# A two-block transformer kernel in eleven stages: products of the identity with itself on TensorE at the changes of stage

## The reference

```python
# first block
h = _rms_norm(x, pre_norm_g)
z_q, z_kv, z_kr, g_attn, u_ssm, g_ssm = split(h @ w_in)
attn = _rms_norm(_mla_attention(z_q, z_kv, z_kr, ...), attn_out_g) * silu(g_attn)
ssm = gelu(_s5_bidirectional(u_ssm, ...))
ssm = _rms_norm(ssm * sigmoid(ssm @ w_glu + b_glu), ssm_out_g) * silu(g_ssm)
x = x + _rms_norm(concat([attn, ssm]) @ w_out, post_norm_g)
# second block (its projections, attention, retention and output product), then
h = modulated(_rmsnorm(x))
p_g, group = top_1(softmax(h @ w_grp + b_grp)); two experts of that group, by softmax
y = sum over the two of weight * ((silu(h @ w_gate[e]) * (h @ w_up[e])) @ w_down[e])
out = _rmsnorm(x + gate * y) * final_g
```

## Time and profile before

| | |
|---|---|
| median of 3 runs | 4364.99 us (4360.97 to 4367.25) |
| the profiled execution | 4367.83 us, its span 4366.0 us |
| mean granted TensorE clock | 0.959 of full |
| busy: PE, DVE, ACT, POOL | 92%, 68%, 56%, 28% |
| PE instructions | 21445 products, as many weight loads |
| from TensorE's last product to the meeting, and from there to the next product | up to 19.2 us together |

### The profile page before, as it was taken

One profiled execution on the slowest core, in us unless ns is written; L12 is line 12 of the kernel. 1 busy time (PEld: TensorE's weight loads), 2 busy tenths in 40 slices (PEclk: granted clock), 3 DMA queues, 4 the chain that ended last, 5 costly groups with the idle time before them and its releaser, 6 DMA issues. The chain is left out here.

```text
span 4366.0 us, 61138 instructions
## 1 busy us (share of the span) xinstructions
PE 4022.8 (92%) x21445; PEld 3412.4 (78%) x21445; DVE 2973.9 (68%) x3831; ACT 2433.6 (56%) x3867; POOL 1231.3 (28%) x846
## 2 busy tenths in 40 slices
PE   8989799999897997999799999997698799999995
PEld 8978689888776876888678888886687588888872
DVE  6667555555486884444477777774655799999985
ACT  6733333333323554333388888887422577777773
POOL 0000145445300110000288888884000111111114
PEclk9999899999998998999899999998899799999998
DMA  6666733333496433222440000004543688888987
GB/s 230 219 212 235 230 113 110 104 118 111 145 287 195 138 105 124 67 67 67 106 163 15 15 23 15 15 10 150 195 155 111 227 319 318 316 321 326 377 318 303
DMA packets 417337, 728.63 MB, mean 167 GB/s; under 512 B 121744, under 2 KB 314384, under 8 KB 396304
## 3 DMA queue, kind: packets, MB, share of 16 engines
q1 hardware_dynamic: 382560, 642.02, 43.0%
q10 hardware_dynamic: 20640, 50.87, 3.3%
q0 software_dynamic: 13968, 33.58, 2.0%
HBM read 601.84 MB, written 213.91 MB: 187 GB/s over the span
## 5 line engine op out<-in xcount | busy, mean ns | idle before, releaser
L2675 POOL TENSOR_TENSOR a_PL<-a_PT,a_PH 128x512 fp32r<-128x512 f32 x512 | 674.4, 1332 | 133.5 <-ACT a_PH L2794 130.3
L2844 DVE TENSOR_REDUCE a_part<-a_pA 128x1 f32<-128x1024 f32 (+1 forms) x384 | 360.0, 955 | 95.4 <-PE a_pA L2698 90.9
L2792 ACT ACTIVATE a_PT<-a_pB 128x512 f32<-128x512 f32 x576 | 340.7, 592 | 78.6 <-PE a_pB L2721 77.3
L2794 ACT ACTIVATE a_PH<-a_PT 128x512 fp32r<-128x512 f32 x576 | 364.4, 633 | 18.4
L3478 POOL DMA_INDIRECT w_XG<-between_h,all_slots x65 | 120.8, 1858 | 779.0 <-PE e_pT L3760 724.8
L1397 ACT ACTIVATE a_PT<-a_pT 128x512 f32<-128x512 f32 x128 | 69.5, 594 | 409.0 <-PE a_pT L1327 409.0
L1432 DVE TENSOR_REDUCE a_maxima<-a_pS 128x1 f32<-128x512 f32 x256 | 176.0, 689 | 132.6 <-PE a_pS L1309 131.1
L1341 PE MATMUL a_pO<-a_V,a_PT 128*128 128x128 f32 x2048 | 249.4, 275 | 1.0 <-DVE a_PT L1445 1.0
L1341 PEld LDWEIGHTS a_pO<-a_V,a_PT 128*128 128x128 f32 x2048 | 243.4, 192 | 6.5 <-DVE a_PT L1445 1.2
L1239 POOL TENSOR_TENSOR a_QL<-a_RQ,a_QT 128x512 fp32r<-128x512 f32 x16 | 20.5, 1284 | 800.6 <-DVE a_QP L1467 800.6
L2739 PE MATMUL a_pO<-a_PL,a_VH 128*128 128x512 f32 x576 | 225.7, 392 | 3.1 <-DVE a_PL L2854 2.1
(11 more groups left out here) (651 smaller groups left out, 10617.5 us busy)
## 6 DMA issues: line engine op xcount, KB each, us to landing
w_gate<-in_moe_w_gate SPq DMA_DIRECT2D x47, 2048.0 KB, 7.7
w_up<-in_moe_w_up SPq DMA_DIRECT2D x47, 2048.0 KB, 12.4
w_down<-in_moe_w_down SPq DMA_DIRECT2D x46, 2048.0 KB
between_yb<-e_Y ACTq DMA_DIRECT2D x46, 512.0 KB, 7.0
a_row_w<-in_w_ada SPq DMA_DIRECT2D x16, 1024.0 KB, 5.5
between_x<-m_X SPq DMA_DIRECT2D x32, 512.0 KB, 2.8
between_yb<-a_zeros SPq DMA_DIRECT2D x32, 512.0 KB, 14.6
between_tv<-pz_OV SPq DMA_DIRECT2D x16, 576.0 KB, 2.9
```

The costliest lines, as they stand in the source:

```text
L2675: pool.tensor_tensor(PL[:, t % RING, :], PT[:, t % RING, :], PH[:, t % RING, :].bitcast(F32), ALU.subtract).then_inc(S["p_low"], 1)
L2792: act.activation(PT[:, t % RING, :], pB[t % 2][:], ACT.Exp, scale=scale).then_inc(S["p_ready"], 1)
L2794: act.activation(PH[:, t % RING, :], PT[:, t % RING, :], ACT.Copy).then_inc(S["p_high"], 1)
L2844: dve.tensor_reduce(part[:, h, r % (NG2 // G4):r % (NG2 // G4) + 1], src, AX_X, ALU.max).then_inc(S["maxed"], 1)
```

## The change

A helper `keep_busy(pe, bank, ident, n)` issues n float32 products of the identity by itself, 128x128 each, into a PSUM bank that is not in use there; nothing waits for them, they wait for nothing, and nobody reads them. Fifteen calls are put in. Seven stand at the head of a PE list, ahead of its first wait: `attention_1` 56, `mix_1` 50, `project_2` 8, `attention_2` 54, `retention` 22, `mix_2` 10, `dispatch` 42. Six stand at the end of a PE list: `project_u` 38, `project_z` 20, `attention_1` 24, `s5` 16, `attention_2` 30, `dispatch` 32. The other two (30 and 56) stand behind a `return` in the helpers `t_stores_before` of `project_2` and `after` of `mix_2`, and issue nothing. The thirteen live calls issue 402 products. No other engine's list changes.

```diff
--- before.py
+++ after.py
@@ -337,6 +337,7 @@
                     products(g, piece, (pU if piece < 2 else pG)[piece % 2], S["mm_u" if piece < 2 else "mm_g"])
                     if piece < GT and g + 1 < NGR:
                         transposed(GT * (g + 1) + piece)
+            keep_busy(pe, pT[0], C["ident"], 38)
 
         @block.scalar
         def _(act):
@@ -846,6 +847,7 @@
             heads(NT - 1)
             gate(NT - 1)
             rope_turned(NT - 1)
+            keep_busy(pe, pA, C["ident"], 20)
 
         @block.scalar
         def _(act):
@@ -1045,6 +1047,12 @@
 
 
 HIGH_BITS = -4096
+
+
+def keep_busy(pe, bank, ident, n):
+
+    for _ in range(n):
+        pe.matmul(bank[:, 0:P], ident[:], ident[:], start=True, stop=True)
 
 
 def high_part(dve, out, x):
@@ -1290,6 +1298,7 @@
 
         @block.tensor
         def _(pe):
+            keep_busy(pe, pO, C["ident"], 56)
             def scores(t, h, g):
                 u = unit(t, h)
                 m = groups[g][1]
@@ -1386,6 +1395,7 @@
             for steps in between:
                 of_unit_before(steps, tile_at(NT), 0)
             row(tile_at(NT - 1))
+            keep_busy(pe, pS[:, 0, :], C["ident"], 24)
 
         @block.scalar
         def _(act):
@@ -1772,6 +1782,7 @@
                         if g % 2:
                             within(h, g)
                         across(h, g)
+            keep_busy(pe, pW[0], C["ident"], 16)
 
         @block.scalar
         def _(act):
@@ -2143,6 +2154,7 @@
 
         @block.tensor
         def _(pe):
+            keep_busy(pe, pG, C["ident"], 50)
             def last_stage(t):
                 i, b = t.i, t.b
 
@@ -2284,6 +2296,7 @@
 
         def t_stores_before(i):
             return 16 * (T_STORES * (i + 1) - 2 * of_context(i))
+            keep_busy(pe, pG, C["ident"], 30)
 
         @block.gpsimd
         def _(pool):
@@ -2345,6 +2358,7 @@
 
         @block.tensor
         def _(pe):
+            keep_busy(pe, pR, C["ident"], 8)
 
             def turned(t):
 
@@ -2676,6 +2690,7 @@
 
         @block.tensor
         def _(pe):
+            keep_busy(pe, pO[0], C["ident"], 54)
             def free(c):
                 if c >= 2:
                     u, r = divmod(c - 2, TURNS)
@@ -2753,6 +2768,7 @@
                     apply(t - LAG)
             for t in range(STEPS - LAG, STEPS):
                 apply(t)
+            keep_busy(pe, pA[0][:, 0, :], C["ident"], 30)
 
         @block.scalar
         def _(act):
@@ -3175,6 +3191,7 @@
 
         @block.tensor
         def _(pe):
+            keep_busy(pe, pX[0], C["ident"], 22)
             def free(c):
                 if c >= 2:
                     h, r = divmod(c - 2, TURNS)
@@ -3274,6 +3291,7 @@
 
         def after(t):
             return Tile(t.i + 1, 1 - t.b, t.n + t.b)
+            keep_busy(pe, pX[0], C["ident"], 56)
 
         @block.gpsimd
         def _(pool):
@@ -3333,6 +3351,7 @@
 
         @block.tensor
         def _(pe):
+            keep_busy(pe, pL, C["ident"], 10)
 
             def transposed(t):
                 pe.wait_ge(S["xh_ready"], t.i + 1)
@@ -3545,6 +3564,7 @@
 
         @block.tensor
         def _(pe):
+            keep_busy(pe, pb, C["ident"], 42)
             pe.wait_ge(S["matrices"], 1)
             pe.wait_ge(S["chosen"], 1)
             m = MM[:].rearrange("p t e -> p (t e)")
@@ -3558,6 +3578,7 @@
                 for j in range(8 * q, 8 * q + 8):
                     mm = pe.matmul(ps[:, 0:NB + 1], in_row[:, j, :], in_block[:, j, :], start=j == 0, stop=j == 2 * NT - 1)
             mm.then_inc(S["listed"], 1)
+            keep_busy(pe, pw, C["ident"], 32)
 
         @block.vector
         def _(dve):
```

## The result

The changed kernel took 4374.1 us, the median of its executions, against 4362.82 us for the kernel before: a ratio of 1.0024, with a 95% interval of 1.0013 to 1.0036. Timed again with twelve executions it took 4376.43 against 4364.29, ratio 1.0024 (1.0014 to 1.0034). It is slower by some 11 us. The forecast was no measurable change, 4363.

A forecast was written before the change was run, and what follows sets the result against it. TensorE, busy 92%, has stage-change pauses the dummies cannot shorten, so only the clock could be won. Ten steps summed to -1.9 us from 4367.83, giving 4365.9; the runs' median being 2.8 lower, 4363 us, 8 in 10 within 4353 to 4371.

The forecast's parts named there:

- The price of a dummy: Time of one added identity product on TensorE: 0.23 us at full clock, 0.43 at half clock.
- Step 1: project_u to project_z: 38 dummies may hold the clock for project_z's first products, -1.5 us (bounds 0 and -2.8).
- the even chance: project_u to project_z: even chances that the clock is held, since a 2 to 3 us pause may or may not cost it.
- Step 2: project_z to attention_1: meeting and loads +1.2 us late, -0.4 from the clock, net +0.8 (bounds -0.6 and +9.7).
- Steps 3 to 6: Changes attention_1 to s5, to mix_1, to project_2, to attention_2: -0.8, 0, 0 and +0.5 us.
- Step 7: attention_2 to retention: 30 and 22 dummies hold the clock, retention's first work speeds up, -2.3 us (bounds 0 and -3.0).
- Step 8: retention to mix_2: a product 1.3 us late, but the clock returns earlier; net -1.0 us (bounds -1.5 and +1.3).
- step 9: mix_2 to dispatch: count products 1.0 us late, 0.5 of it returned; net +0.4 us (bounds -0.5 and +7.1).
- Step 10: dispatch to experts: 32 dummies end late and delay experts' start, products gain nothing; +2.0 us (bounds -4.5 and +5.8).
- the ceiling of 30.6 us: Behind eleven pauses TensorE works 61.3 us at half clock; a clock held up could give 30.6 us, 0.7% of the span.
- Rival A: The clock holds across all ten changes and TensorE paces what follows: -23.4 us, 4341.6 us; chance 0.08.
- Rival B: Dummies do not raise the clock, run at 0.43 us and overrun their pauses: +42.7 us, 4407.7 us; chance 0.05.

The follow-up runs named there:

- g4: The kernel before with only the 38 dummies behind project_u; 4369.2 us, ratio 1.0005.
- f2: The changed kernel with its first five calls alone (project_u, project_z, both of attention_1, s5); 4369.81 us, ratio 1.0017.
- h4: The kernel before with 10 dummies of 512 columns behind project_u alone, the work of the 38; 4363.8 us, ratio 0.9991.
- h1: The changed kernel with a never-taken branch of 402 dummies ahead of the loop in TensorE's program of experts; 4381.67 us, ratio 1.0037.
- g3: The changed kernel without the 20 dummies behind project_z and the 42 ahead of and 32 behind dispatch; 4378.07 us, ratio 1.0031.
- g1: The changed kernel with each call's n products of 128 columns replaced by n/4 of 512 columns; 4372.84 us, ratio 1.0018.
- g2: The changed kernel with each dummy replaced by four increments of a semaphore nobody reads; 4500.78 us, ratio 1.0307.
- f4: The kernel before with only the 30 dummies behind attention_2 and the 22 ahead of retention; 4367.02 us, ratio 1.0008.
- e2: The kernel before with only the 32 dummies behind dispatch's last products; 4365.56 us, ratio 1.0003.

## Why the prediction was wrong

By its steps, with what two profiles of the changed kernel and the single-cause runs showed:

- **The price of a dummy** (0.23 us, 0.43 at the lower level): right. 38 took 8.64 (8.7 forecast), 20 4.63 (4.6), 24 5.52 (5.5), 42 11.92 (12.0), 10 3.95 (4.3), 54 13.64 (14.8), 32 9.17 (9.7). Only the 8, wholly at the lower level, took 3.75, over their bound of 3.4.
- **Step 1**, -1.5: here the forecast failed first. The start is faster: the first cast comes 1.1 us earlier against the first product in both profiles of the changed kernel, no more than in the kernel before's second profile, but 2.7 in g4 and f2, where the clock held; the even chance was fair. But 2.7 to 3.0 us are lost behind it, which with h4's run (no such loss with the same work in 20 matmul records) is the instructions' doing: a piece of them arrives while a store of the stage is under way, and the store takes 4.5 us in place of 2.9. The step said that project_z's next products follow directly on its first, and had no term for the rest of the stage.
- **Step 2**, +0.8: the meeting was late by 1.5 and 1.7 (1.2 forecast). Attention_1 then took 2.1 us more in both profiles and in f2 and h1, 2.5 in g3, which lacks the 20. So this part is not the late meeting. Nor is it the wait for `a_PR`, though that is 5.26 us in place of 3.79 before: it ends 10.1 us behind the first product, against 10.4. Most of it, 1.6 us, is lost in the last 8 us of the stage, where the clock falls. Before and after (stretch, length, TensorE's busy time and records, granted clock, DMA share, GB/s):

```profile
1170.70:1178.70 8.00, 6.34 (x53) 1.00 0.74 253
1176.60:1184.60 8.00, 6.67 (x42) 0.79 0.99 330
```

The second profile of the kernel before has 0.79 there too, so this isn't the dummies' alone; it made it good at the stage's start, where the clock held and it was 1.8 us faster. In g1, with wide dummies, the clock stays at 1.00 and the stage is 2.1 us shorter. In g2, with as many instructions and no work, the stage takes what it took before, so the number of instructions is not shown to lengthen it. What makes the clock fall there stays open.
- **Steps 3 to 6**, -0.8, 0, 0, +0.5: nothing beyond the noise. The first product of attention_2 was 0.3 late in one profile and 1.8 in the other (1.7 forecast), and its window still shows 0.66, as the step had feared of so thin a stream.
- **Step 7**, -2.3: from first product to scan the changed kernel's first profile is faster by just that, 2.30 us, but its first product came 1.6 later on `r_V`, so that 0.7 was left; in the second the first product came 3.0 later and only 0.4 of it returned. The step missed that load as the next thing to be late, and that a piece of instructions can fall into its flight. Alone (f4) the pair is not faster.
- **Step 8**, -1.0, and **step 9**, +0.4: mix_2's first transpose 0.7 late behind the stage's start, its last product 0.8 and 1.6 earlier; dispatch's first product 0.7 and 1.1 late, 0.5 of it returned. Right.
- **Step 10**, +2.0: +1.37 and +1.57, and +1.39 alone in e2, all against the first profile of the kernel before; against its second 0.3 less. Right in kind, a little high.
- **What no step had**: experts. A term for it stands nowhere, neither in the sum nor among the rivals. It is 6.8 us by the averages above, the greatest part of the 11, and 8.4 between the two profiles of each kernel.

So the step that failed is one that all ten share. The sum goes over the changes of stage and counts for each how late the meeting comes and what the first products save. Everything behind them it takes as unchanged, at 0 and without a reason. The 1608 added instructions as such were taken to cost nothing beyond the dummies' own time. The runs showed 6.8 us in experts and some 3 in project_z that follow the instructions and not the work. With these two terms the forecast of -1.9 would have been +7.9.

The tally: 6.8 in experts, some 3 in project_z, 1.6 at attention_1's start and 2.1 within it, and 1.5 at experts' start are 15.0, where the medians differ by 11.3. These items are read from profiled executions, and those of the two kernels differ by 15.6 and 15.5. So the tally is a rough one, and what the faster starts gave back isn't measured by itself. Of the ceiling of 30.6 us that is little: most stages' starts are paced by loads and casts, as the forecast had it. Rival A needed TensorE to pace them. Rival B is refuted: the clock rose under the dummies wherever they were many (1.00 at 1389.20 and 3011.00). The Trainium skill's rule on products in transpose mode (TensorE: Matmul & The Clock Gate, Part 4) found no use here, since dummies are plain products, and no run here shows it.

## What to carry to other kernels

An instruction that does nothing is not free even where its engine is idle: it moves the whole stream behind it, and stages far away, bound by transfers, can pay. If a pause is to be filled at all, take few wide products, which did no harm in project_z, and not many narrow ones, which did, and only where the first work behind it waits for nothing but TensorE can it pay; here no such filling gained anything clear of noise. When a load or a store takes longer than before, look for a piece of instructions in its flight. When a stage that wasn't touched gets slower, compare the count of instruction pieces in the two profiles before looking for a cause in the stage, and time the edit again with padding that does no work.

## What was not expected of the hardware

A 16 KB piece of TensorE's instructions lengthens a transfer in whose flight it begins: a store of 576 KB from 2.9 to 4.5 us in the median (251 and 53 issues), a load of 1152 KB from between 5.3 and 6.0 to between 7.2 and 9.5 us (14 and 5 profiles). The piece is 16 KB, and why it costs so much is not shown.

The steps of a loop for which TensorE fetches no code (no piece of its instructions arrives between 3487 and 4325 us in the changed kernel), and which is paced by 2 MB loads, depend on how many 16 KB pieces of TensorE's instructions were fetched before it: 12 to 20 steps slow at 94 pieces, 29 to 31 at 100, 13 at 110. The load of `w_up` takes 12.6 to 12.8 us at 100, by the page's median, and 12.3 to 12.5 at 94. It would fit if the pieces were dealt out to the 16 DMA engines in turn and their number decided how a later load falls on them; the profile doesn't name the engine of a packet, so this is a guess. Padding the stream to the good count was not tried as a way to make the kernel faster.

A granted clock between its two levels is on record as well. The run with 512 dummies has it over project_z and the most part of attention_1, with work that is the kernel before's to the instruction. The same stretch of attention_1 there and in the kernel before:

```profile
700.00:1180.00 480.00, 478.43 (x3258) 0.95 0.35 108
697.80:1177.80 480.00, 478.35 (x3285) 1.00 0.36 110
```

TensorE got through 0.8% fewer products in it, not 5%. From its first to its last products attention_1 took 2.45 us longer there, and project_z 1.7 against the first profile of the kernel before and 2.9 against the second. One such execution among the profiled ones is a reason to want a distance in several profiles.
